# Two changes to a two-block transformer kernel: where the split products of a gated feed-forward are added, and where the conditioning weights stand in the weight stream

## The reference

```python
def swiglu(x, w_gate, w_up, w_down):                 # layer of the first block, twice
    return (jax.nn.silu(x @ w_gate) * (x @ w_up)) @ w_down

cond = jax.nn.silu(c)                                # second block
for i in range(2):
    mod = (cond @ ada_w[i] + ada_b[i])[:, None, :]   # six vectors of 1024 a layer
    sh1, sc1, g1, sh2, sc2, g2 = jnp.split(mod, 6, axis=-1)
    h = rmsnorm_2(x, norm1_g[i]) * (1.0 + sc1) + sh1
    y = sliding window attention (i = 0) or stick-breaking attention (i = 1) of h
    x = x + g1 * y
    h = rmsnorm_2(x, norm2_g[i]) * (1.0 + sc2) + sh2
    x = x + g2 * swiglu_2(h, w_gate[i], w_up[i], w_down[i])
```

## Time and profile before

| | us |
|---|---|
| median of 3 runs | 1188.81 |
| the runs | 1187.91, 1188.81, 1193.43 |
| the profiled execution, its own time | 1186.83 |
| its span, first to last instruction | 1185.1 |

### The profile page before, as it was taken

How to read it: one execution, slowest core, us unless ns; L and a number is a source line. 1 busy time by engine, 2 the same in 40 slices (tenths; PEclk the granted TensorE clock), 3 DMA queues, 4 the chain that set the end, 5 groups by cost and what they waited for, 6 DMA issues and landing times.

```text
span 1185.1 us, 16903 instructions
## 1 busy us (share of the span) xinstructions
PE 1152.3 (97%) x6614; PEld 994.1 (84%) x6614; DVE 872.7 (74%) x1180; ACT 641.4 (54%) x1010; POOL 212.3 (18%) x230
## 2 busy tenths in 40 slices
PE   6999999999999999999898999999999999999998
PEld 5888888899999888888676788888878988888887
DVE  6565856545457779999876678999987757677664
ACT  5553645466656554454566554454555775654551
POOL 0221220000002012455332012222220001121210
PEclk9999999999999999999999999999999999999999
DMA  9553754754444579999741347999958533576640
GB/s 346 206 189 132 257 203 143 262 201 157 158 148 143 195 268 304 354 355 367 271 156 56 108 160 241 342 367 368 333 204 317 188 115 110 214 279 219 252 152 36
DMA packets 42238, 262.97 MB, mean 222 GB/s; under 512 B 7344, under 2 KB 7728, under 8 KB 12336
## 3 DMA queue, kind: packets, MB, share of 16 engines
q1 hardware_dynamic: 42160, 261.90, 61.1%
HBM read 260.78 MB, written 1.10 MB: 221 GB/s over the span
## 4 chain that ended last, share of the span: by engine, by line
PE 64%; DVE 20%; DMA 7%; ACT 4%; issue 3%; POOL 2%; SPq 0%; DVEq 0%; POOLq 0%; ACTq 0%
PE ps L340 61%; DVE wl L973 8%; DVE raw L982 6%; DMA raw<-in_stream 5%; DMA vectors<-small 2%; ACT wh L1525 1%; DVE arena L1140 1%; PE ps L526 1%; PE ps L903 1%; DVE hl L1113 1%; PE ps L706 1%; POOL small L1906 1%; DVE x L1008 0%; POOL arena L1932 0%; DVE xn L1078 0%
## 5 line engine op out<-in xcount | busy, mean ns | idle before, releaser
L973 DVE TENSOR_TENSOR wl<-raw,wh 128x1024 fp32r<-128x1024 f32 x374 | 499.1, 1356 | 42.3 <-ACT wh L1525 41.3
L1525 ACT ACTIVATE wh<-raw 128x1024 fp32r<-128x1024 f32 x374 | 388.6, 1052 | 130.0 <-DMA raw<-in_stream 108.2
L340 PE MATMUL ps<-x,wh 128*128 128x512 f32 (+1 forms) x1984 | 445.3, 347 | 0.0
L340 PEld LDWEIGHTS ps<-x,wh 128*128 128x128 f32 x1984 | 342.4, 190 | 45.1 <-issue 3.4
L340 PE MATMUL ps<-x,wl 128*128 128x256 f32 x1568 | 264.7, 282 | 0.0
L340 PEld LDWEIGHTS ps<-x,wl 128*128 128x128 f32 x1568 | 236.7, 191 | 11.3
L340 PE MATMUL ps<-wh,x 128*128 128x512 f32 (+1 forms) x600 | 183.9, 384 | 2.4 <-DVE x L1008 2.3
L340 PE MATMUL ps<-wl,hh 128*128 128x512 f32 x404 | 159.1, 394 | 2.5 <-DVE wl L973 2.5
L340 PE MATMUL ps<-wh,hh 128*128 128x512 f32 x404 | 159.5, 395 | 1.4 <-ACT arena L1829 1.4
L340 PE MATMUL ps<-wh,hl 128*128 128x512 f32 x404 | 157.6, 390 | 0.0
L340 PEld LDWEIGHTS ps<-wh,x 128*128 128x128 f32 x600 | 111.9, 190 | 24.4 <-issue 2.2
(11 more groups left out here) (179 smaller groups left out, 826.0 us busy)
## 6 DMA issues: line engine op xcount, KB each, us to landing
raw<-in_stream SPq DMA_DIRECT2D x233, 1024.0 KB, 5.5
arena<-vectors SPq DMA_DIRECT2D x12, 512.0 KB, 6.1
arena<-in_tables SPq DMA_DIRECT2D x7, 576.0 KB, 6.2
raw<-in_stream SPq DMA_DIRECT2D x4, 512.0 KB, 8.5
gain_sb<-in_gains SPq DMA_DIRECT2D x3, 512.0 KB, 7.9
res<-in_x SPq DMA_DIRECT2D x4, 256.0 KB, 5.0
out_dram<-res SPq DMA_DIRECT2D x3, 256.0 KB, 2.0
gain_sb<-in_gains SPq DMA_DIRECT2D x2, 256.0 KB, 5.2
```

The lines of the kernel that those rows point to most:

```text
L340: return e.matmul(o, a, b, start=start, stop=stop)
L973: e.tensor_tensor(WL[:, n % NW, :], src, WH[:, n % NW, :].bitcast(F32), ALU.subtract).then_inc(*w_lo.tick(n))
L1525: e.activation(WH[:, m % NW, :], src, ACT.Copy).then_inc(*w_hi.tick(m))
```

## The change

**Where parts are added.** ScalarE now copies only the x-low part of the gate (256 columns) and, new, of the up tile (256 columns, behind the Silu). VectorE adds each to the part that is still in PSUM (two new additions of 256 columns) and multiplies the two sums (256 columns instead of 512). GpSimd has no part in feed-forwards any more. The gate's bank is now freed by VectorE's addition, not by ScalarE's copy. The rotary tables are made by GpSimd in one go.

**Where ada units stand.** 24 of them (vectors 0 to 2) go to feed-forward 0, 32 (vectors 3 to 6) stay in or move to feed-forward 1, and 24 (vectors 7 to 9) stay in feed-forward 2. `cond` is loaded and put through Silu twice, at group 7 and again for feed-forward 1. Vectors 0, 1, 2, 5 and 6 come back from DRAM at later fixed places. The remaining edits put SyncE's other loads at places counted from their stage.

```diff
-        ffn_units(0) + mix
-        + spread(ffn_units(1), ada_units(0, 5))
+        spread(ffn_units(0), ada_units(0, 3)) + mix
+        + spread(ffn_units(1), ada_units(3, 7))
         + swa
-        + spread(ffn_units(2), ada_units(5, 10))
+        + spread(ffn_units(2), ada_units(7, 10))
...
+    back_after = {g + 1: v for g, v in out_after.items()}
+    for v, place_ in ((0, second_at + 7), (1, second_at + 8), (2, second_at + 9), (5, raw_place["tm", "gu2", 4] // GROUP + NRAW),
+                      (6, raw_place["tm", "gu2", 6] // GROUP + NRAW)):
+        back_after = {g: x for g, x in back_after.items() if x != v} | {place_: v}
...
-            if g == 5:
+            if g == 7:
                 sp.wait_ge(*vec.of("out", 0, 1, 1))
+                e.dma_start(cond, io["c"].partition_broadcast(P)).then_inc(*c_in.tick(0))
+            if g == mixer_at + 7:
+                sp.wait_ge(*ada.of(2, KT - 1))
                 gain("norm_ffn2")
...  TensorE: banks
-                evicted[b] = [acted.of("gate", i, j)]
+                evicted[b] = [vec.of("gate", i, j)]
...
-                evicted[b] = [vec.of("prod", i, j)]
+                evicted[b] = [vec.of("up", i, j)]
...  VectorE
+                dv.wait_ge(*acted.of("gate part", i, j))
...
+                e.tensor_tensor(gate_sum[j % 2], gate_part[j % 2], bank(place["fm", g, j], S), ALU.add).then_inc(
+                    *vec.tick(("gate", i, j)))
                 at(N["fm", u, j])
-                dv.wait_ge(*acted.of("silu", i, j))
-                dv.wait_ge(*formed.of("fm", u, j))
+                dv.wait_ge(*acted.of("up part", i, j))
...
-                e.tensor_tensor(parts(prod_parts[j % 2]), parts(bank(place["fm", u, j])),
-                                silu[j % 2].unsqueeze(1).to_broadcast([P, 2, S]), ALU.mult).then_inc(*vec.tick(("prod", i, j)))
+                e.tensor_tensor(up_sum[j % 2], up_part[j % 2], bank(place["fm", u, j], S), ALU.add).then_inc(
+                    *vec.tick(("up", i, j)))
                 if j > 4:
                     h_low(j - 1)
+                dv.wait_ge(*acted.of("silu", i, j))
...
+                e.tensor_tensor(prod[j % 2], silu[j % 2], up_sum[j % 2], ALU.mult).then_inc(*vec.tick(("prod", i, j)))
...  ScalarE
-            if i == 1:
-                ac.wait_ge(*c_in.of())
-                e.activation(cond, cond, ACT.Silu).then_inc(*acted.tick(("cond",)))
+            if i < 2:
+                ac.wait_ge(*c_in.of(i))
+                e.activation(cond, cond, ACT.Silu).then_inc(*acted.tick(("cond", i)))
...
-                e.activation(gate_parts[j % 2], bank(place["fm", g, j]), ACT.Copy).then_inc(*acted.tick(("gate", i, j)))
+                e.activation(gate_part[j % 2], bank(place["fm", g, j], S, S), ACT.Copy).then_inc(*acted.tick(("gate part", i, j)))
...
-                ac.wait_ge(*pooled.of("gate", i, j))
+                ac.wait_ge(*vec.of("gate", i, j))
...
+                ac.wait_ge(*formed.of("fm", u, j))
...
+                e.activation(up_part[j % 2], bank(place["fm", u, j], S, S), ACT.Copy).then_inc(*acted.tick(("up part", i, j)))
...
-                ac.wait_ge(*pooled.of("prod", i, j))
+                ac.wait_ge(*vec.of("prod", i, j))
...  GpSimd: feed_forward(i) with its two additions a block, and rotary(step), are gone
+        for t in range(2):
+            cos, sin = trig[:, 16 * t:16 * t + 8], trig[:, 16 * t + 8:16 * t + 16]
+            for h0, n, g in ((0, 16, head_gain[:, 0:16]), (16, 2, head_gain[:, HD:HD + 16])):
+                for i, (x, part) in enumerate(((cos, 0), (sin, 8), (cos, 8), (sin, 0))):
+                    z = e.tensor_tensor(TURN[t][:, i, h0:h0 + n, :], x.unsqueeze(1).to_broadcast([P, n, 8]),
+                                        g[:, part:part + 8].unsqueeze(1).to_broadcast([P, n, 8]), ALU.mult)
+        z.then_inc(*pooled.tick(("tables",)))
```

More of the change, by code:

```diff
@@ L212, in program @@
     prod = [AR(512 + 256 * i, 256) for i in range(2)]
-    gate_parts = [AR(3072 + 512 * i, 512) for i in range(2)]
-    prod_parts = [AR(1024 + 512 * i, 512) for i in range(2)]
-    gate_sum = [AR(4096 + 256 * i, 256) for i in range(2)]
+    gate_part, up_part = ([AR(1024 + 512 * x + 256 * i, 256) for i in range(2)] for x in range(2))
+    gate_sum, up_sum = ([AR(3072 + 512 * x + 256 * i, 256) for i in range(2)] for x in range(2))
     BOTH = AR(6016, D)
@@ L978, in condition @@
             dv.wait_ge(*there)
-            dv.wait_ge(*acted.of("cond"))
+            dv.wait_ge(*acted.of("cond", 0 if v < 3 else 1))
             dv.wait_ge(*column_in.of("all"))
@@ L1968, in gpsimd @@
         e.memset(small_pair, 1.0).then_inc(*pooled.tick(("pair",)))
-        feed_forward(1)
+        po.wait_ge(*turn_in.of("all"))
+        for c, factor in ((q_scale, -1.0), (k_scale, 8.0)):
+            e.tensor_scalar(c, c, factor, None, ALU.mult)
+        e.tensor_scalar(neg_sink, neg_sink, -1.0, None, ALU.mult).then_inc(*pooled.tick(("sinks",)))
+        po.wait_ge(*vec.of("trig"))
+        for t in range(2):
[5 more added lines that the diff above has]
+        z.then_inc(*pooled.tick(("tables",)))
         for t in range(2):
@@ L2009, in gpsimd @@
         turned_heads(8)
-        for t in range(2):
-            gated_sum(4, t)
-            power(4, t)
-        feed_forward(2)
-        for t in range(2):
-            gated_sum(5, t)
-            power(5, t)
+        for q in (4, 5):
+            for t in range(2):
+                gated_sum(q, t)
+                power(q, t)
         e.memset(unseen, 0.0).then_inc(*pooled.tick(("unseen zero",)))
```

71 lines of the change are left out of this document (23 added, 48 removed).

## The result

| | before | after |
|---|---|---|
| median of 4 runs each, same chip | 1191.12 us (1187.91 to 1195.71) | 1177.98 us (1177.62 to 1178.79) |
| ratio after / before, 95% interval | | 0.9888 [0.9849, 0.9926] |
| profiled execution: own time | 1186.83 us | 1178.79 us |
| profiled execution: span | 1185.1 us | 1177.1 us |
| mean granted clock of TensorE | 0.997 | 0.999 |

The kernel became 1.1% faster. The forecast was 1180.3 us in a range of 1175 to 1189, so the time lies in the range and 2.3 us under the forecast. The runs after lie within 1.2 us of each other, those before within 7.8 us. Three of the four runs before are the ones that the forecast started from (median 1188.81 us); the fourth, 1195.71 us, moved their median up.

A forecast was written before the change was run, and what follows sets the result against it. TensorE was taken to bound the kernel, with gains only where it waits. Terms 3.5 + 2.0 + 1.6 + 1.4 = 8.5 us, taken from the median 1188.81, gave 1180.3 us, range 1175 to 1189.

The forecast's parts named there:

- That only TensorE's waits can be won: Feed-forwards: TensorE sets the pace, so VectorE or GpSimd load is worth nothing while VectorE stays within its 13.7 us lead.
- The block's cost on VectorE: Feed-forward block on VectorE: 8.7 us before; after, 6.7 in feed-forwards 0 and 2, 7.4 in 1; TensorE needs 8.2.
- (a): Near the end of feed-forward 1: TensorE's six waits for low halves go, 3.5 us, bounds 2.5 and 4.
- (b): Boundary behind feed-forward 1: VectorE, 2.05 us late with the second residual sum, catches up; the gap falls by 2.0 us.
- (c): After the gap behind feed-forward 1: TensorE's clock no longer falls to half, 1.6 us back, bounds 0 and 1.7.
- (d): Boundary behind feed-forward 2: the second sum came 2.1 us late; the 1.4 us wait at the transposes goes.
- The scale: Whole kernel: 1178.3 us for an execution like the profiled one; the median lies 2.0 us above it, so 1180.3 us.
- The DMA rival: Feed-forward 1: DMA, not VectorE, held it; only 2.4 us won, 1186.4 us; chance 0.19.
- The rotary burst: Feed-forward 1: 16 GpSimd operations, forecast 8.5 us of lag; rival: full length, 20 us, time 1186.3 us, chance 0.06.
- The hand-off rival: Feed-forwards: VectorE's three steps a block each wait for ScalarE, 1.2 us a step, making it slower, 1207 us; chance 0.10.
- The gate's bank at block 4: Bank freed by VectorE's addition, margin 0.7 us: cost 0, up to 0.7 us at each of four feed-forwards.
- `cond` in feed-forward 0: ScalarE's Silu of it, about 1.05 us, fits an idle stretch of 2.34 us: nothing, or up to 2 us if late.

The follow-up runs named there:

- the experiment with chosen gaps: Changed kernel with 7, 10 and 14 unneeded VectorE instructions ahead of the transposes at three boundaries, so that TensorE waits there: 1188.63 us, one run.
- part 1 alone: Kernel before with GpSimd's additions moved to VectorE and the ada units left where they were: 1177.8 us, ratio 0.9924.
- part 2 with the added load: Kernel before with the change's unit list and SyncE places, GpSimd still adding, plus two unneeded VectorE operations a block in feed-forward 1: 1183.85 us, ratio 0.9968.
- the late return: Kernel before with each conditioning vector fetched back four groups after it went out instead of one: 1186.94 us, ratio 0.9991.
- 26 instructions: Changed kernel with 26 unneeded VectorE operations of 256 columns in block 14 of feed-forward 1: 1178.62 us, one run.
- product on VectorE: Changed kernel with the product of residual and final norm's gain behind feed-forward 1 on VectorE instead of GpSimd: 1177.05 us, ratio 0.9912.
- the burst: Changed kernel with 56 unneeded VectorE operations of 256 columns in block 14 of feed-forward 1: 1193.78 us, one run.

## Why the prediction held, point by point

- **That only TensorE's waits can be won** held. In every stretch of a feed-forward with ada units TensorE started 134 or 135 matmuls in 25 us, before and after, though VectorE's busy time fell by 1.5 us at 475 us and by 4.2 at 775.
- **The block's cost on VectorE** held for the kernel after: 20.7 / 25 x 8.2 = 6.8 us in feed-forward 2, where 6.7 was forecast, and 22.07 / 25 x 8.2 = 7.2 us in feed-forward 1, where 7.4 was. For the kernel before the sum of the lag was put together wrongly: 7 us from the blocks and up to 8.5 from the rotary steps made 15.5, and nothing was put in for late units. Measured it was 12.0 at block 19, 2.6 of it in waits for units, and so 9.4 for all of VectorE's work, rotary steps with it.
- **(a), the waits for low halves,** had the right mechanism and the wrong size: 4.4 us measured, 3.5 taken, with 4 as the upper bound. The six waits were the right six, and the profile names 2.5 us of idle time for them. I gave each 0.16 us on top for the modelled end of the matmul before. By TensorE's starts the first three cost 0.16 us on top and the last three 0.28 to 0.30, 3.8 us in sum; 0.6 us more lie in the matmuls just behind a wait, as delays that leave no idle time, and my addition had no term for them.
- **(b), the boundary behind feed-forward 1,** measured 2.04 us, taken 2.0. **(c), the clock,** measured 1.71, taken 1.6 with 1.7 as the bound; the experiment with chosen gaps gave the same sign (no fall after 2.0 us, 2.3 us lost after 4.81). **(d)** measured 1.51, taken 1.4. The way to (b) and (d), by which a place where VectorE waits serves as the yardstick for one where it is late, gave both within about 0.1 us.
- **The scale** was the larger part of the 2.3 us between forecast and median. The sum gives 1178.3 us for an execution like the profiled one. The profiled execution after took 1178.79 us, but that nearness is luck: the sum was 1.4 us too small (9.9 against 8.5), and this execution started 1.9 us late. Two others without the late start took 1177.21 and 1176.38 us. Between medians the change was worth 13.1 us in the result and 10.9 and 10.0 us beside the experiments, all of them more than 8.5. I set 2.0 us on top, since the median before lay that much over its profiled execution. That offset was part of what the change removed: the kernels that stay within the lead ran from 1176.4 to 1178.8 us, save for one execution of part 1 alone, while the kernel before ran from 1183.0 to 1195.7. That the spread of the kernel before comes from its place at the edge of the lead, where a late transfer or a collision more is paid in full, fits much of this, but was only argued: there is no profile of a run at 1195 us. Against it stands part 2 with the added load, which is past its lead too and spread over 2.1 us only, in five runs; it has the lighter stream, so late units may be what spreads the runs before.
- **The DMA rival** fell as the main account of feed-forward 1 (part 1 alone keeps the stream and loses the waits; the added load keeps the light stream and has them). It has a share in the kernel before, the 2.6 us of waits for late units. It is real at another place and now and then, as the execution of 1181.8 us shows. My forecast of a DMA share below 0.9 in feed-forward 1 missed: it was 0.98 at 475 us and 0.93 at 525. The stream is uneven, and I had reckoned with its mean from there on only; over the whole of 425 to 575 us it is (before, then after)

```profile
425.00:575.00 150.00, 148.84 (x792) 127.88 (x791) 143.85 (x171) 75.10 (x107) 61.01 (x55) 1.00 0.89 327
```

```profile
425.00:575.00 150.00, 150.00 (x800) 129.60 (x799) 132.52 (x198) 82.73 (x133) 14.51 (x19) 1.00 0.90 321
```

nearly the same share and GB/s, with VectorE 11.3 us less busy, and TensorE without idle time.
- **The rotary burst** was neither the 8.5 us of the forecast nor the 20 of the rival. GpSimd ran its 16 operations in one piece:

```profile
476.52 12.00 POOL L1965 TENSOR_TENSOR arena<-small 128x128 f32<-128x128 f32 x16
```

0.75 us each, in place of the 1.23 by which I had bounded them, and the low halves beside them grew little: in feed-forward 1 the shortest, the median and the longest of 55 are these:

```profile
L982 DVE TENSOR_TENSOR wl<-raw,wh x55: 1216/1220/1478, 427.9 to 573.2; 128x1024 fp32r<-128x1024 f32 x55
```

At 0.26 us for the worst, 16 of them cost VectorE at most 4.2 us. On its timeline from 476 to 489 us the delays, with those on an ada unit and on a product, come to 1.2 us.

The three other collisions on a timeline can be set beside the rule that the prediction weighed. What was left of GpSimd's instruction when VectorE's began, and what VectorE's took longer: 0.67 and 0.53 us, 0.55 and 0.42 (the product above), 0.32 and 0.18 (the low half above). The Trainium skill, "SBUF — State Buffer", section "Who interferes with whom", has the engine that comes first hold the shared read interface for the whole instruction. The three agree with it but for some 0.13 us each. The rotary burst does not: by it a low half that starts beside one of those instructions, 0.75 us each and one right behind the other, would be held up by up to 0.75, and none was by more than 0.26.
- **The hand-off rival** fell: VectorE's idle time before its 72 gate sums, 52.3 us for ScalarE (first fence of this part of the document), is large, and TensorE paid nothing for it. They are waits that VectorE has time for. The same holds for the Silu row that spoke for that rival.
- **The gate's bank at block 4** and **`cond` in feed-forward 0** were costed at nothing. No wait of TensorE at block 4 or in feed-forward 0 for either is in the trace after.

## What to carry to other kernels

Where one engine feeds another through a ring of buffers, write its work per block beside the consumer's, multiply the difference by the blocks in which it lasts, and compare with the ring's depth in time (here 13 us). Below it load cost next to nothing here, and two remedies that each took the lag under it did not add up. Look in the producer's own idle times for late input: it adds to the lag. Take the price of a boundary from the same step at a boundary where the feeding engine was early, and read the saving on the starts of the bound engine, since idle times behind a modelled end miss the small delays; and where the old kernel stands at its edge, don't carry its median's distance from the profiled run over to the new one.

## What the runs showed of the hardware that I had not expected

- **The clock** fell to 0.50 after idle times of TensorE of 2.60 us (part 1 alone), 2.83 (before), 4.81 and 13.84 us, and not after 1.36, 1.53, 1.56, 2.0, 2.1 or 2.2 us, nor after 2.37 (the late return). Each profiled execution, of every kernel here, also has a wait of 2.60 or 2.61 us in sliding-window attention, and the clock fell behind it every time, for 3.4 us in most and for 6.8 in three (26 instructions, gaps, product on VectorE). After 13.84 us it was at half for 13.6 us, 8.8 of them still in the wait. At the boundaries and the burst the price was 1.65 to 2.4 us.
- **A collision** with GpSimd costs whichever two-operand VectorE instruction it meets: 0.18 and 0.53 us on low halves, 0.42 us on a product that takes 0.42 alone. Why the 16 rotary operations cost a low half no more than 0.26 us stays open; no run was made on it.
- **GpSimd** took 0.73 and 0.61 us, in the timeline shown, for a product of 256 columns for which VectorE took 0.46 (25.69 / 56) when nothing ran beside it on GpSimd.
